# A ring of six places for the experts' weights, and the product keys' gate table moved from GpSimd to VectorE

## The reference, cut to what matters

```python
# block 1, each token to its 4 best experts (softmax over the 4 logits)
gu = xb @ w_gu[e] + b_gu[e]                  # 1024 -> 2048
y  = clamped_swiglu(gu) @ w_down[e] + b_down[e]   # 1024 -> 1024

# block 2, product keys: 8 heads, for each the 16 best of 128 keys on either
# side, then the 16 best of the 256 sums; softmax over these gives the gates
# G[token, i * 128 + j] = sum over heads of the gate of the pair (i, j)
# y = sum over i, j of G * gelu(h . u[i, j]) * v[i, j]
```

## Time and profile before

| | |
|---|---|
| median of three runs | 3379.26 us (3374.78 to 3379.70) |
| profiled execution | 3371.07 us |
| its span | 3369.3 us |
| TensorE busy | 3013.5 us, 89% |
| VectorE busy | 1281.4 us, 38% |
| ScalarE busy | 867.9 us, 26% |
| GpSimd busy | 127.3 us, 4% |
| moved by DMA | 763.9 MB |

### The profile page before, as it was taken

How to read it: one execution, slowest core, us unless ns; L and a number is a source line. 1 busy time by engine, 2 the same in 40 slices (tenths; PEclk the granted TensorE clock), 3 DMA queues, 4 the chain that set the end, 5 groups by cost and what they waited for, 6 DMA issues and landing times.

```text
span 3369.3 us, 55104 instructions
## 1 busy us (share of the span) xinstructions
PE 3013.5 (89%) x21350; PEld 2375.7 (71%) x21350; DVE 1281.4 (38%) x2809; ACT 867.9 (26%) x1464; POOL 127.3 (4%) x85
## 2 busy tenths in 40 slices
PE   7999899999999999988999518899999999889998
PEld 5678655555455454547788417799999999767887
DVE  1520212122221222222411589866666666521330
ACT  2310112212222222221411004444444444321110
POOL 0000000000000000000000016500000000000000
PEclk9999889999999999999999759999999999879999
DMA  5664579999999999984654200045545555423342
GB/s 233 263 252 155 197 297 386 398 385 392 397 386 397 389 384 398 377 360 152 236 221 142 88 0 0 0 167 182 187 176 185 183 178 186 164 75 125 138 150 88
DMA packets 105299, 763.89 MB, mean 227 GB/s; under 512 B 11776, under 2 KB 11776, under 8 KB 12672
## 3 DMA queue, kind: packets, MB, share of 16 engines
q1 hardware_dynamic: 103536, 753.97, 58.3%
q0 software_dynamic: 1680, 8.72, 0.7%
HBM read 760.55 MB, written 2.10 MB: 226 GB/s over the span
## 4 chain that ended last, share of the span: by engine, by line
PE 79%; DMA 9%; DVE 8%; issue 2%; ACT 1%; DVEq 0%; POOL 0%; SPq 0%; ACTq 0%; POOLq 0%
PE psum L554 20%; PE psum L793 13%; PE psum L1163 11%; PE psum L1172 11%; DMA weight_ring<-in_stream 9%; PE psum L751 4%; PE psum L822 3%; DVE chunkbuf L1887 3%; PE psum L1229 2%; PE psum L570 2%; PE psum L761 2%; PE psum L516 2%; PE psum L545 1%; PE psum L772 1%; DVE work L1293 1%
## 5 line engine op out<-in xcount | busy, mean ns | idle before, releaser
L793 PE MATMUL psum<-weight_ring,work 128*64 128x256 f32 x4224 | 494.5, 384 | 37.0 <-DMA weight_ring<-in_stream 36.2
L554 PE MATMUL psum<-hT,weight_ring 128*128 128x256 f32 x2240 | 505.0, 388 | 15.5 <-ACT hT L2049 15.5
L554 PEld LDWEIGHTS psum<-hT,weight_ring 128*128 128x128 f32 x2240 | 436.0, 195 | 80.9 <-issue 18.7
L793 PEld LDWEIGHTS psum<-weight_ring,work 128*64 128x64 f32 x4224 | 290.0, 137 | 226.5 <-DMA weight_ring<-in_stream 78.9
L1548 DVE TENSOR_TENSOR work<-psum,work 128x256 f32<-128x256 f32 x132 | 56.2, 426 | 810.6 <-PE psum L772 810.6
L822 PE MATMUL psum<-weight_ring,work 128*64 128x512 f32 x1056 | 248.2, 602 | 28.7 <-DMA weight_ring<-in_stream 28.4
L1172 PE MATMUL psum<-peer_parts,v_high 128*128 128x256 f32 x2048 | 266.8, 283 | 0.3 <-DVE ring_parts L1942 0.2
L1172 PEld LDWEIGHTS psum<-peer_parts,v_high 128*128 128x128 f32 x2048 | 254.9, 192 | 0.7 <-DVE ring_parts L1942 0.7
L822 PEld LDWEIGHTS psum<-weight_ring,work 128*64 128x64 f32 x1056 | 66.6, 136 | 186.8 <-DMA weight_ring<-in_stream 96.8
L554 PE MATMUL psum<-work,weight_ring 128*128 128x256 f32 x800 | 175.9, 382 | 5.4 <-DVE work L1293 3.0
L1922 DVE TENSOR_TENSOR chunkbuf<-chunkbuf,work 128x256 f32<-128x256 f32 x128 | 81.7, 638 | 240.0 <-ACT chunkbuf L2324 240.0
(11 more groups left out here) (251 smaller groups left out, 3626.1 us busy)
## 6 DMA issues: line engine op xcount, KB each, us to landing
weight_ring<-in_stream SPq DMA_DIRECT2D x719, 1024.0 KB, 6.5
work<-in_rows POOLq DMA_DIRECT2D x1, 1312.0 KB, 16.9
xT<-in_x POOLq DMA_DIRECT2D x1, 1024.0 KB, 9.8
work<-in_ctx POOLq DMA_DIRECT2D x1, 1024.0 KB, 18.9
x_spill<-xT POOLq DMA_DIRECT2D x1, 1024.0 KB, 7.4
xT<-x_spill POOLq DMA_DIRECT2D x4, 256.0 KB, 6.8
out_x<-xT POOLq DMA_DIRECT2D x4, 256.0 KB, 2.9
work<-in_moe POOLq DMA_DIRECT2D x1, 768.0 KB, 6.7
```

The lines of the kernel that those rows point to most:

```text
L554: mm = pe.matmul(ps[:, j * T:(j + 1) * T], w[:, c, j * P:(j + 1) * P], moving[:, c, :], start=(j == 0 and c == 0), stop=True, skip_group_c ...
L793: mm = pe.matmul(psum[g * SEATS:(g + 1) * SEATS, 4 + i % 2, 0:256], m["xe"][:, 4 * h + c, :], w[:, c, g, :], start=(h == 0 and c == 0), st ...
```

## The change

**Experts.** The ring gets two more places (`MORE = 2`) in the last 4096 elements of `work`, used only by the experts' pieces. Within an item piece j goes to place j % 6 of six; the four old ones are used in the order in which the pieces before would have met them. `place_of`, `slot`, `landed` and `landed_of` give a piece's place and the count that says it has landed. SyncE's new `item` sends the twelve pieces of an item: a piece waits until the piece six before it is used. For the first item pieces 0 to 3 wait as before, and 4 and 5, whose places are empty, don't wait. Outside the experts the ring has four places as before.

**Product keys.** The table `bd` is made by VectorE in `gate_blocks`, with the same operands, right after the one-hot `oh2` of the same chunk. GpSimd makes nothing here any more. The rest of the diff is names.

```diff
+MORE = 2
...
+        more = work[:, 32768 - MORE * SLOT:32768].rearrange("p (s k) -> p s k", s=MORE)
+        loads = 12 // (SLOTS + MORE)
+        def place_of(n):
+            if moe_at <= n < moe_end:
+                s = (n - moe_at) % 12 % (SLOTS + MORE)
+                return s if s >= SLOTS else (moe_at + s) % SLOTS
+            return n % SLOTS
+        def slot(n):
+            s = place_of(n)
+            return ring[:, s, :] if s < SLOTS else more[:, s - SLOTS, :]
...
+        def landed_of(n, e):
+            full, count = landed(n)
+            return full, e * (16 * loads) + count
...
-                            pe.wait_ge(ring_full[n % SLOTS], e * 48 + 16 * (n // SLOTS + 1))
-                            w = ring[:, n % SLOTS, :].rearrange("p (c g o) -> p c g o", c=4, g=2)
+                            pe.wait_ge(*landed_of(n, e))
+                            w = slot(n).rearrange("p (c g o) -> p c g o", c=4, g=2)
...
+            def item(at_once, piece_of, e=0):
+                for j in range(12):
+                    n = moe_at + j
+                    if at_once and j >= SLOTS + MORE:
+                        sp.wait_ge(used.sem, n - (SLOTS + MORE) + 1)
+                    elif at_once and j < SLOTS:
+                        sp.wait_ge(used.sem, n - SLOTS + 1)
+                    elif not at_once:
+                        sp.wait_ge(used.sem, e * 12 + (n - (SLOTS + MORE) + 1))
+                    sp.dma_start(slot(n), piece_of(j)).then_inc(landed(n)[0], 16)
...
-                sent(SLOTS, again, 0)
+                sent(SLOTS, moe_at, 0)
+                item(True, lambda j: stream[moe_at + j])
+                with sp.Fori(1, E_N) as e:
+                    item(False, lambda j: stream[e * 12 + (moe_at + j)], e)
                 sp.wait_ge(*at("flag_set"))
                 fullest = sp.value_load(A[1]["flag"][0:1, 1:2], min_val=0, max_val=E_N - 1)
...
+                item(False, lambda j: stream[fullest * 12 + (moe_at + j)], E_N)
+                sent(moe_end, n_pieces, 12)
...
+                    def gate_blocks(s, at0):
+                        ve.tensor_tensor(m["bd"][s].rearrange("p k (h a) -> p k h a", h=8),
+                                         m["gT"][:, :, bass.ds(at0, CHUNK)].rearrange("p a k -> p k a").unsqueeze(2)
+                                         .to_broadcast([P, CHUNK, 8, 16]),
+                                         m["v"]["head_mask"].unsqueeze(1).unsqueeze(3).to_broadcast([P, CHUNK, 8, 16]),
+                                         ALU.mult).then_inc(tok_p[t], 1)
...
                         for s in range(2):
                             ve.wait_ge(tok_e[t], i * 4 + (2 * s - 3))
                             onehot(1, m["oh2"][s], i * (2 * CHUNK) + CHUNK * s)
+                            gate_blocks(s, i * (2 * CHUNK) + CHUNK * s)
                             ve.wait_ge(tok_e[t], i * 4 + (2 * s - 1))
                             onehot(0, m["oh1"][s], i * (2 * CHUNK) + CHUNK * s)
...
-                    with gp.Fori(1, P // CHUNK // 2) as i:
-                        for s in range(2):
-                            gp.wait_ge(tok_e[t], i * 4 + (2 * s - 3))
-                            block(s, i * (2 * CHUNK) + CHUNK * s)
-                gp.wait_ge(tok_p[1], P // CHUNK)
+                gp.wait_ge(*at("gT_sb1"))
```

More of the change, by code:

```diff
@@ L247, in table, with landed @@
             return got
-        ring_full = [sem(f"ring_full_{s}") for s in range(SLOTS)]
+        ring_full = [sem(f"ring_full_{s}") for s in range(SLOTS + MORE)]
+        moe_at = first_piece["moe"]
+        moe_end = moe_at + 12 * ITEMS
+        more = work[:, 32768 - MORE * SLOT:32768].rearrange("p (s k) -> p s k", s=MORE)
+        assert moe_at % SLOTS == moe_end % SLOTS and 12 % (SLOTS + MORE) == 0
+        loads = 12 // (SLOTS + MORE)
[7 more added lines that the diff above has]
+            return ring[:, s, :] if s < SLOTS else more[:, s - SLOTS, :]
+        def landed(n):
+            s = place_of(n)
+            if n < moe_at:
+                return ring_full[s], 16 * (n // SLOTS + 1)
+            past = len([k for k in range(moe_at) if k % SLOTS == s]) if s < SLOTS else 0
+            if n < moe_end:
+                e, j = divmod(n - moe_at, 12)
+                return ring_full[s], 16 * (past + loads * e + j // (SLOTS + MORE) + 1)
+            return ring_full[s], 16 * (past + loads * ITEMS + (n - moe_end) // SLOTS + 1)
+        def landed_of(n, e):
+            full, count = landed(n)
+            return full, e * (16 * loads) + count
         used = signal("pieces_used")
@@ L503, in piece @@
                 n = place[name, i]
-                pe.wait_ge(ring_full[n % SLOTS], 16 * (n // SLOTS + 1))
-                return ring[:, n % SLOTS, :]
+                pe.wait_ge(*landed(n))
+                return slot(n)
             def conditioning(s, a, b, fresh=False):
@@ L816, in narrow @@
                         n = base + 8 + k
-                        pe.wait_ge(ring_full[n % SLOTS], e * 48 + 16 * (n // SLOTS + 1))
+                        pe.wait_ge(*landed_of(n, e))
                         pe.wait_ge(nar_act, e * 4 + (k + 1))
-                        w = ring[:, n % SLOTS, :].rearrange("p (f o) -> p f o", f=2)
+                        w = slot(n).rearrange("p (f o) -> p f o", f=2)
                         for f in range(2):
@@ L1257, in send @@
                 sp.wait_ge(used.sem, n - SLOTS + 1)
-                sp.dma_start(ring[:, n % SLOTS, :], stream[k]).then_inc(ring_full[n % SLOTS], 16)
+                sp.dma_start(slot(n), stream[k]).then_inc(landed(n)[0], 16)
             def sent(first, last, back):
@@ L1907, in u_low @@
                 def u_low(s):
-                    slot = (first_piece["peer"] + s) % SLOTS
-                    ve.tensor_tensor(ring_parts[:, slot, 0:D], ring[:, slot, 0:D], m["u_high"][:, s % 2, :].bitcast(F32), ALU.subtract) \
+                    at0 = (first_piece["peer"] + s) % SLOTS
+                    ve.tensor_tensor(ring_parts[:, at0, 0:D], ring[:, at0, 0:D], m["u_high"][:, s % 2, :].bitcast(F32), ALU.subtract) \
                       .then_inc(blk_ul, 1)
@@ L1938, in block @@
                     ve.tensor_tensor(low, wt, high.bitcast(F32), ALU.subtract).then_inc(blk_w, 1)
[L1940 removed]
+                    at0 = (first_piece["peer"] + s) % SLOTS
                     ve.wait_ge(blk_h, n + 1)
[L1942 removed]
+                    ve.tensor_tensor(ring_parts[:, at0, D:2 * D], ring[:, at0, D:2 * D], m["v_high"][:, s % 2, :].bitcast(F32), ALU.subtract) \
                       .then_inc(blk_w, 1)
@@ L2333, in u_high, with in_ring @@
                       .then_inc(blk_uh, 1)
-                def landed(s):
-                    return ring_full[(base + s) % SLOTS], 16 * ((base + s) // SLOTS + 1)
-                sc.wait_ge(*landed(0))
+                def in_ring(s):
+                    return landed(base + s)
+                sc.wait_ge(*in_ring(0))
                 u_high(0)
                 for s in range(4):
-                    sc.wait_ge(*landed(s + 1))
+                    sc.wait_ge(*in_ring(s + 1))
                     if s >= 1:
@@ L2351, in peer @@
                     for s in range(4):
-                        full, count = landed(s + 1)
+                        full, count = in_ring(s + 1)
                         sc.wait_ge(full, i * 16 + count)
@@ L2361, in peer @@
                     if s < 3:
-                        sc.wait_ge(*landed(n + 1))
+                        sc.wait_ge(*in_ring(n + 1))
                         sc.wait_ge(blk_a, n)
```

20 lines of the change are left out of this document (2 added, 18 removed).

## The result

The changed kernel takes 3275.48 us (median of 4 runs, 3267.8 to 3277.6) against 3377.02 us before in the same comparison: ratio 0.9695, 95% interval [0.9676, 0.9715], 103 us less (96 to 109). The forecast was 3311 us with a range from 3290 to 3342: the direction and the place were right, the size was not, and the time lies under the range.

What follows compares the result with a forecast made beforehand. The prediction took the experts to be held by the four-place ring coupling TensorE and the weight stream, and VectorE to pace the product keys; -66 - 2 = -68 us from the median 3379.3 gave 3311 us, range 3290 to 3342.

Steps and rivals of the forecast that it cites:

- the term for an item with six places: Experts: an item takes the larger of 29.9 and 29.8 us plus 0.3 for stream unevenness, 30.2 us instead of 32.25.
- 29.88 us for TensorE: Experts: TensorE's work in one item without waits, summed from timeline durations, against 29.8 us for the stream.
- the head start: First expert item: two additional pieces are ordered 5 us of transfer earlier, in an idle stretch; nothing added to the gain.
- upper end for the gain: Experts: the most the ring could bring, 32 x 2.35 = 75 us, against 66 forecast and 40 at the lower end.
- The product keys: Filling loop: with the table on VectorE, a period goes from 4.85 to 4.80 us, 2 us less over 32 periods.
- the hole of 240 GB/s: Experts, 1031 to 1037 us: the stream drops from 424 to 240 GB/s, losing 2.6 us of transfer in each item.
- the count behind it: Experts' ring: 2.0 pieces ready, one in use, one covering the order time; claimed over four and under six places.
- Rival (1): Experts: the stream doesn't hold 424 GB/s without pause, an item stays at 31.0 us or more; 3337 us, chance 0.12.
- Rival (2): Experts: the ring does nothing, an unseen limit holds an item at 32.2 us; 3377 us, chance 0.03.
- (4): Product keys: the table on VectorE costs 1.85 us or so; 3355 us, chance 0.03.
- (5): Product keys: the strided, twice broadcast product is much dearer, slower than before from 2.25 us; 3402 us at 2.6, chance 0.03.
- Rival (3): Product keys: the table on VectorE costs as a free one-hot, 0.69 us; 3298 us, chance 0.09.

## Why the prediction was wrong, step by step

**The failed step** is the term for an item with six places, "I take 0.3, near the low end", which gave 30.2 us, and the bound behind it, 29.88 us for TensorE. The item measured is 29.80 us, set by the stream, and 29.39 in the first four, where TensorE sets it. Up to the last down piece the change won 81.7 - 1.7 = 80.0 us against 66 forecast. The 14 us between them are, to some tenths:

- 32 x 0.40 = 12.8 us. The allowance of 0.3 us for unevenness rested on no row and is zero: with enough on order the stream keeps 422 GB/s for 940 us. The other 0.1 is the distance from the sum of 29.88, rounded up, to the true bound.
- 4 x 0.41 = 1.6 us in the first items. The prediction gave the head start nothing.
- 1.5 us at the last four down pieces, 6.1 us where they took 7.6 with two waits for pieces. Against these stands the start, 1.7 us later.

TensorE's 29.88 added durations of groups that overlap. The second item of the changed kernel waits for no piece:

```profile
473.85 3.67 PE L827 MATMUL psum<-weight_ring,work 128*64 128x256 f32 x32
...
490.47 3.65 PE L856 MATMUL psum<-weight_ring,work 128*64 128x512 f32 x16
493.96 3.60 PE L856 MATMUL psum<-work 128*64 128x512 f32 x16
497.39 3.62 PE L827 MATMUL psum<-weight_ring,work 128*64 128x256 f32 x32
500.94 2.00 PE L795 MATMUL psum<-work 64*128 64x256 f32 x16
...
503.24 3.67 PE L827 MATMUL psum<-weight_ring,work 128*64 128x256 f32 x32
```

From start to start the four down pieces take 497.39 - 490.47 = 6.92 us where the forecast had 7.30, and pieces 0 and 1 take 3.55 where it had 3.67; with 490.47 - 473.85 = 16.62 and 503.24 - 500.94 = 2.30, both as forecast, that is 29.39. The error put TensorE's bound above the stream's. So the prediction named TensorE as what is late next, and it is the stream; and its upper end for the gain, 75 us, was no bound.

**The product keys** were priced at -2 us and brought -9. The mechanism held: one-hots at 0.69, the period explained by the same chain, the table's wait as the last one. Sizes were off: 1.04 us for the table (1.11 forecast), and an instruction overlaps the next by 0.08 us and not 0.05, so three take 2.25 us and not 2.39; the hand-overs are 0.28 and not 0.36. I also gave the step of the gates as 1 KB (in the description too); `gT` has 128 tokens a row, so it is 512 bytes, the very step of L1922. That made the neighbour row fit better than I said.

**The medians.** The forecast was tied to one profile. In that profile the old experts took 1039.8 us, and the old kernel was 6 us under its median, while the changed one lay 1 us under its own. A gain read from that profile is short. Of the 35.5 us by which the forecast was off, 28.6 are in the profiles (14.0 in the experts, 7.1 in the product keys, 7.5 in stretches that nobody changed), the other 6.9 lie between profile and medians. The two errors of the sum alone move the forecast to 3290 us, the edge of its range. The rest is not the change's: of all the profiles the first of the kernel before has the longest last part (1184.6 us) and the changed kernel's the shortest (1180.1).

Right were: that both sides had room and the ring's depth held them; the hole of 240 GB/s as cause, shown by the orders held back to four; that six places are enough and four are not, though the count behind it says four; no fall of the clock at 97% busy; no cost on GpSimd or SyncE that any profile shows. Rival (1), a stream that does not hold 424 GB/s, fell: it holds 422. Rival (2) fell with it, as did (4) and (5) by 1.04 us. Rival (3) was wrong as named, since the step costs 0.35 us, but the result lay on its side.

## What to carry to other kernels

Where two sides are each nearly full and a ring ties them, find what each would need alone, from start-to-start times and from a stretch at full rate; if both are under the measured time, the ring's depth is the bound, and one more place can be worth all of it. Count the places: pieces ready at the start of the fastest burst, one in use, and one for an order's own time. Here this count gave 4.0 and five were needed, so take it as a lower bound and try one more; the sixth brought 2.6 us. Don't add an allowance for unevenness that no row shows; put it into the range. A two-heaped duration (0.69 and 1.83 us) is a wait in disguise: price the instruction by its lower heap. Add up start-to-start times, not listed durations: the overlap was 0.5 us in an item of 29.4.

## What the runs showed of the hardware

- A stream of 1 MB pieces into all 128 partitions held 422 GB/s for 940 us, with TensorE 97% busy beside it. Which of two arrays a piece went to made no difference.
- A VectorE product of 128x512 float32 with two SBUF inputs takes 0.69 us, 1.04 when one input is read with a step of 512 bytes. A copy of the same size out of PSUM takes 0.69 us in order and 1.00 when it writes with a step of 64 bytes.
- A one-hot on VectorE, both inputs in SBUF, that started beside a product on GpSimd took 1.83 us in place of 0.69, about as long as GpSimd's product (1.85); moving that product to VectorE, at 1.04 us, made the loop faster than having it for nothing on another engine.
- The soonest landing came 4.7 us after its order (7.3 in the median with four on order). With six on order the median was 10.2 us for pieces into `weight_ring` and 9.1 for those into `work`, and the stream ran at 422 GB/s.
- The middle part of the kernel, the same in all, had 128 to 145 us at half clock and took 502 to 509 us.
